# A fourth one-time place for an expert weight block, in room taken from the scratch of dynamic DMAs

## Chip, cores and metric

The kernel runs on one core of a Trainium2 chip. The metric is device time in microseconds (us) of one execution, taken as the median of several runs. The core has a matrix engine (TensorE, PE in the profile), three engines for elementwise work (VectorE or DVE, ScalarE or ACT, GpSimd or POOL) and SyncE (SP), which here only asks for DMA transfers. All transfers run on the core's 16 DMA engines between the large off-chip memory (HBM) and the on-chip memory (SBUF).

## What is computed

One inference step of a decoder layer for 256 prompt tokens and 8 sample tokens with width 1024: a combined projection, a gated delta rule for one group of heads and latent attention for the other, an output projection, cross attention over 256 memory tokens, and a mixture of 32 experts. Cut to the two stages that matter here:

```python
def cross_attend(hn, mem_k, mem_v, w_xq, w_xo):
    q = (hn @ w_xq).reshape(B, T, X_HEADS, X_HEAD_DIM)
    s = jnp.einsum('bthd,bmhd->bhtm', q, mem_k).astype(jnp.float32) * (X_HEAD_DIM ** -0.5)
    p = jax.nn.softmax(s, axis=-1).astype(mem_v.dtype)
    return jnp.einsum('bhtm,bmhd->bthd', p, mem_v).reshape(B, T, -1) @ w_xo

def moe_ffn(h, w_router, b_router, w_e1, b_e1, w_e2, b_e2):      # 32 experts, top 4
    ...
    def expert(acc, ew):
        hh = xt @ w1 + b1
        glu = jnp.minimum(hh[:, 0::2], SWIGLU_LIMIT)
        lin = jnp.clip(hh[:, 1::2], -SWIGLU_LIMIT, SWIGLU_LIMIT)
        y = ((lin + 1.0) * (glu * jax.nn.sigmoid(SWIGLU_ALPHA * glu))) @ w2 + b2
        return acc + g_col[:, None].astype(y.dtype) * y, None
```

For the 8 sample tokens, the cached keys and values of the latent attention are gathered through a page table, and each sample has its own cross-attention keys and values of 1 MB (`cache_mem_k`, `cache_mem_v`).

## The kernel before

The program is a chain of blocks with a barrier of all engines between them. Each engine's instructions are written out in order and tied to the others by semaphores. SBUF is one large tensor, `arena`, whose places are reused by hand, with a few small tensors beside it.

**Gathers.** `load_sequence` (L410) has POOL issue two indirect DMAs for each of 8 samples: the latent rows and the rotary-key rows, 128 descriptors each. Three places take the 8 sequences in turn, so a gather waits until the sequence before it in its place has been used.

**Cross attention of the samples** is in the last block (L1951). PE turns the keys of sample n into columns (`turn_keys`, two steps m for each sample, L2104) and scores them (`score`, L2112). Keys of samples 0 to 3 were loaded in the block before; those of samples 4 to 7 go into the same four places, and SP asks for each when the sample in its place has been scored (L1958). The expert biases are asked for between them (L1961, L1962), and then the values of samples 4 to 7 (L1965).

**Experts.** They go in 16 pairs. The weights of a pair are 24 fills of 1 MB each (128 partitions by 2048 floats): fills 0 to 15 are the first matrix of the two experts, 16 to 23 the second. Even fills belong to the first expert of the pair, odd ones to the second. PE uses them in order, two at a time: `hidden` (L2039) fills 0 to 15, `output` (L2076) fills 16 to 23. A pair takes 16 x 24 = 384 fills in all.

Fills go into a ring of 12 places. Three of the first pair's fills, 21 to 23, have one-time places outside the ring (`spare`, L1889), which other data holds before or afterwards. SP asks for the fills of the first pair as their places become free of earlier data: fill 0 in the block before, fill 3 as the first instruction of the last block (L1954), 8 to 11, 4 to 7, 1 and 2 as the cross attention gives up its buffers, 21 and 22 when the last projection is done, and 23 after the third set of router logits. From then on SP waits, before each fill, on the semaphore that PE raises when the place has been used:

```python
            for n in range(RING, FIRST_SPARE):
                sp.wait_ge(free[n % RING], 1)
                fill_first(sp, n)
            ...
            for n in range(RING):
                fill_later(1, n, 2)
```

`slot_of` and `uses` (L1910 to L1914) give the ring place of a fill in the later pairs and how often that place has been filled; both depend on `SPARE`, the number of one-time places.

Of the kernel before, what the change touches and what calls it, by code (L numbers as in the profile page):

```python
# [53 lines left out]
C_HEAD = C_SUB + 1  # L54
C_ALL = C_HEAD + H

ARENA = 45680

CACHED = (PAST // P) * (KVR + ROPE)
AT_WIN, AT_HEADS, AT_HIST = 0, 22528, 44032  # L60
# [82 lines left out]
def build(nc, x_prompt, x_sample, state_gdn, state_conv, cache_latent, cache_krope, page_table,  # L143
# [7 lines left out]
    def sem(name, lasting=False):  # L151
        s = nc.alloc_semaphore(name)
        if not lasting:
            recent.append(s)
        return s
# [7 lines left out]
    def keep(name, shape, dt=F32):  # L163
        return nc.alloc_sbuf_tensor(name, shape, dt)
# [4 lines left out]
    xnT = keep("xnT", [P, KD, TOK])  # L169
    arena = keep("arena", [P, ARENA])  # L170
    small = keep("small", [P, 64])
# [10 lines left out]
    def store(eng, dst, src):  # L182
        n_stored[0] += 16
        eng.dma_start(dst, src).then_inc(stored, 16)
# [260 lines left out]
    with nc.Block() as block:  # L445
        @block.sync
        def _(sp):
            for t in range(2):
                sp.dma_start(res[:, t, :], x_prompt[0, t * P:(t + 1) * P, :]).then_inc(tile_loaded[t], 16)
            sp.dma_start(res[0:DEC, 2, :], x_sample[:, 0, :]).then_inc(tile_loaded[2], 16)  # L450
            for k in range(KD):
                sp.dma_start(win[:, k, :], w_in[0, k * P:(k + 1) * P, :]).then_inc(w_in_loaded[k], 16)
            sp.dma_start(hist, state_conv[0].rearrange("b j c -> (b j) c")).then_inc(hist_loaded, 16)
            sp.dma_start(cst[:, P:C_ALL], const_f32[:, P:C_ALL]).then_inc(const_loaded, 16)

            sp.wait_ge(hist_moved, 1)
            sp.dma_start(pgi, page_table.rearrange("b j -> j b"), allow_slow_non_contiguous=True).then_inc(ml["pages"], 16)
            sp.dma_start(kvn[:, :], kv_norm[0].partition_broadcast(P)).then_inc(ml["kvn_loaded"], 16)
            sp.dma_start(alog[:, :], a_log[0].partition_broadcast(P)).then_inc(decay_loaded, 16)
            sp.dma_start(dtb[:, :], dt_bias[0].partition_broadcast(P)).then_inc(decay_loaded, 16)  # L460
            sp.dma_start(uq, w_uq[0].rearrange("(k p) h n -> p k h n", p=P)).then_inc(ml["uq_loaded"], 16)

            store(sp, conv_sample[0, :, 0:2, :], state_conv[0, :, 1:3, :])
            sp.wait_ge(tail_moved, 3)
            store(sp, conv_prompt[0, 0], tail[0:3, :])
            store(sp, conv_sample[0, :, 2, :], tail[3:3 + DEC, :])
            sp.wait_ge(ml["lat_ready"], NT)
            store(sp, lat_prompt[0, 0].rearrange("(t p) n -> p t n", p=P), rest[:, 0:2, CKV0:CKV0 + KVR])
            store(sp, lat_sample[:, 0, 0, :], rest[0:DEC, 2, CKV0:CKV0 + KVR])
            store(sp, kr_prompt[0, 0].rearrange("(t p) n -> p t n", p=P), kr[:, 0:2, :])  # L470
            store(sp, kr_sample[:, 0, 0, :], kr[0:DEC, 2, :])
            sp.wait_ge(rest_proj, 7)
            sp.dma_start(uk, w_uk[0].rearrange("(k p) h n -> p k h n", p=P)).then_inc(ml["w_loaded"], 16)
            sp.dma_start(uv, w_uv[0].rearrange("(k p) h n -> p k h n", p=P)).then_inc(ml["w_loaded"], 16)
            sp.wait_ge(stored, n_stored[0])
# [851 lines left out]
    AT_WK, AT_MEMT, AT_MV, AT_WOUT, AT_WV, AT_WXQ, AT_WXO = 0, 8192, 10240, 12288, 20480, 28672, 36864  # L1327
# [129 lines left out]
    def fill(sp, n, e, place, landed):  # L1457

        x = n % 2
        if n < 16:  # L1460
            k = n // 2
            src = w_e1[0, bass.ds(e + x, 1), k * P:(k + 1) * P, :].rearrange("a p n -> (a p) n")
            sp.dma_start(place, src).then_inc(landed, 16)
        else:
            k = 2 * ((n - 16) // 2)
            src = w_e2[0, bass.ds(e + x, 1), k * P:(k + 2) * P, :].rearrange("a (k p) n -> p (a k) n", p=P)
            sp.dma_start(place.rearrange("p (k n) -> p k n", k=2), src).then_inc(landed, 16)  # L1467

    def fill_first(sp, n):
        fill(sp, n, 0, ring[n % RING], full[n % RING])  # L1470
# [413 lines left out]
    AT_YE = late_moe.at  # L1884
    ye = late_moe.take([P, D])
    assert AT_YE + 2048 <= AT_WXO + KD * D
    SPARE = 3
    FIRST_SPARE = FILLS - SPARE
    spare = (xnT[:, :, :].rearrange("p k n -> p (k n)")[:, 0:2048], arena[:, AT_YE:AT_YE + 2048], arena[:, AT_WOUT + 2048:AT_WOUT + 4096])  # L1889
    spare_full = [sem(f"spare{i}_full") for i in range(SPARE)]  # L1890
    spare_used = sem("spare_used")
    left = (left_0, left_1, left_s)
# [17 lines left out]
    def slot_of(n):  # L1910
        return (n - SPARE) % RING

    def uses(it, n):
        return it * 2 + (n // RING + (0 if n % RING < SPARE else 1))  # L1914

# [22 lines left out]
    def wait_y(eng, it):  # L1938

        if type(it) is int and it == 0:  # L1940
            eng.wait_ge(spare_used, SPARE)
        else:
            eng.wait_ge(free[slot_of(23)], uses(it, 23))

    def n_rounds(eng):
        return eng.value_load(rounds[0:1, 0:1], min_val=1, max_val=MAXR)
# [4 lines left out]
    with nc.Block() as block:  # L1951
        @block.sync
        def _(sp):
            fill_first(sp, 3)  # L1954
            sp.wait_ge(stored, memory_stored)
            for b in range(G):
                sp.wait_ge(sx["scored"], b + 1)
                sp.dma_start(Kx[:, b], cache_mem_k[0, G + b].rearrange("(s p) h n -> p s (h n)", p=P)).then_inc(kx_loaded[b], 16)  # L1958
                if b > 0:
                    part = slice((b - 1) * NE, b * NE)  # L1960
                    sp.dma_start(bias[part, 0:2 * D], b_e1[0]).then_inc(mo["b_loaded"], 16)  # L1961
                    sp.dma_start(bias[part, 2 * D:3 * D], b_e2[0]).then_inc(mo["b_loaded"], 16)  # L1962
            for b in range(G):
                sp.wait_ge(sx["scored"], G + b + 1)
                sp.dma_start(Kx[:, b], cache_mem_v[0, G + b].rearrange("(s p) h n -> p s (h n)", p=P)).then_inc(kx_loaded[b], 16)  # L1965
            sp.dma_start(wr, w_router[0].rearrange("(k p) n -> p k n", p=P)).then_inc(mo["r_loaded"], 16)
            sp.dma_start(br, b_router[0].partition_broadcast(P)).then_inc(mo["r_loaded"], 16)
            sp.dma_start(pick, const_bf16).then_inc(mo["pick_loaded"], 16)
            sp.wait_ge(sx["out"], 1)
            for n in range(8, RING):  # L1970
                fill_first(sp, n)
            sp.wait_ge(sx["out"], 2)
            for n in range(4, 8):
                fill_first(sp, n)
            sp.wait_ge(mo["bias_ready"], 1)
            for n in (1, 2):
                fill_first(sp, n)
            sp.wait_ge(mo["made"], 5)
            for i in range(2):
                fill(sp, FIRST_SPARE + i, 0, spare[i], spare_full[i])  # L1980
            sp.wait_ge(mo["logits"], 3)
            fill(sp, FIRST_SPARE + 2, 0, spare[2], spare_full[2])

            sp.wait_ge(mo["rounds"], 1)
            sp.wait_ge(mo["parts_ready"], NT + 1)
            sp.dma_start(nf, norm_final.partition_broadcast(P)).then_inc(fn["gain"], 16)
            nr = n_rounds(sp)
# [4 lines that stand above are left out]
            def fill_later(it, n, e):  # L1992
                sp.wait_ge(free[slot_of(n)], uses(it, n) - 1)
                fill(sp, n, e, ring[slot_of(n)], full[slot_of(n)])

            for n in range(RING):
                fill_later(1, n, 2)
            with sp.Fori(1, nr * PAIRS - 1) as it:
                e = sp.snap((it % PAIRS) * 2)
                after = sp.snap(((it + 1) % PAIRS) * 2)  # L2000
                for n in range(RING, FILLS):
                    fill_later(it, n, e)
                for n in range(RING):
                    fill_later(it + 1, n, after)
            final = last_pair(sp)
            for n in range(RING, FILLS):
                fill_later(final, n, NE - 2)
            sp.wait_ge(fn["done"], 1)
            store(sp, y_sample[:, 0, :], res[0:DEC, 2, :])
            for t in range(2):  # L2010
                for n in range(2):
                    sp.wait_ge(fn["done"], 2 + 2 * t + n)
                    store(sp, y_prompt[0, t * P:(t + 1) * P, n * 512:(n + 1) * 512], res[:, t, n * 512:(n + 1) * 512])
            sp.wait_ge(stored, n_stored[0])
# [707 lines left out]
```

## Time and profile before

| | before |
|---|---|
| runs | 1494.47, 1496.4, 1496.8 us |
| median | 1496.4 us |
| profiled execution, span from first to last instruction | 1494.2 us |
| PE busy | 1373.9 us (92%) |
| moved by DMA | 490.73 MB, 328 GB/s over the span |

The page gives the profiled execution's span and no other time of it; the lowest of the runs is 0.3 us above that span, the median 2.2 us. Times in the rows are from the start of the span. SPq is SP's queue of DMA issues. The share of DMA is that of all 16 DMA engines; it can be over 1 in a short stretch, since packets are counted where they start.

### The profile page before, as it was taken

How to read it: one execution, taken by the hardware profiler on the slowest of the kernel's cores; microseconds unless marked ns; L12 is line 12 of the kernel's file. 1: busy time of each engine (PE TensorE's matmuls, PEld its weight loads, DVE VectorE, ACT ScalarE, POOL GpSimd, SP SyncE). 2: the span in 40 equal slices, each digit the busy share in tenths (PEclk: the TensorE clock that was granted, in tenths of full speed). 3: DMA queues.
4: the chain of work that ended last, by engine and by line, in shares of the span. 5: the costliest groups of instructions: out<-in, count | busy, mean ns of one | idle time of the engine just before them, and what ended most of it. 6: DMA issues, size and time to landing. Idle time of an engine off the chain costs nothing.

```text
span 1494.2 us, 21159 instructions
## 1 busy us (share of the span) xinstructions
PE 1373.9 (92%) x8579; PEld 694.5 (46%) x8579; DVE 460.2 (31%) x1116; ACT 201.1 (13%) x399; POOL 42.6 (3%) x37
## 2 busy tenths in 40 slices
PE   8999899899998989999999988989989889899896
PEld 7668766555486453333333333333433333333332
DVE  1856643553024252113113112111221131122213
ACT  1053322321012440000000000000000000000002
POOL 0000101000000320000000000000000000000000
PEclk9999999999999989999999999999999999999999
DMA  9111534448365669999999999999999999999996
GB/s 367 39 53 57 199 143 149 184 150 329 141 253 180 225 276 413 389 413 424 426 425 424 428 425 424 427 424 426 425 424 429 423 424 426 424 426 427 424 426 245
DMA packets 96727, 490.73 MB, mean 328 GB/s; under 512 B 9307, under 2 KB 14527, under 8 KB 61626
## 3 DMA queue, kind: packets, MB, share of 16 engines
q1 hardware_dynamic: 94074, 468.89, 76.8%
q0 software_dynamic: 2304, 20.97, 3.6%
q8 instruction: 39, 0.64, 0.2%
q10 hardware_dynamic: 296, 0.11, 0.0%
q14 instruction: 14, 0.11, 0.0%
HBM read 484.01 MB, written 6.04 MB: 328 GB/s over the span
## 4 chain that ended last, share of the span: by engine, by line
PE 40%; DMA 18%; DVE 6%; issue 2%; SPq 1%; ACT 1%; POOL 1%; DVEq 0%
PE ps L2039 17%; DMA arena<-in_w_e 17%; PE ps L2076 14%; PE ps L2032 2%; PE ps L2064 1%; DVE arena L2604 1%; DVE arena L2614 1%; DVE arena L2611 1%; PE ps L2088 1%; DVE arena L2612 1%; SPq L1467 1%; DMA arena<-in_cache_mem_k 1%; PE ps L2104 1%; PE ps L2118 1%; PE ps L2112 0%
## 5 line engine op out<-in xcount | busy, mean ns | idle before, releaser
L2039 PE MATMUL ps<-arena 128*64 128x512 f32 x2048 | 454.3, 595 | 22.1 <-DMA arena<-in_w_e 21.5
L2039 PEld LDWEIGHTS ps<-arena 128*64 128x64 f32 x2048 | 148.9, 137 | 303.5 <-issue 278.5
L2076 PE MATMUL ps<-arena 128*64 128x512 f32 x952 | 214.2, 604 | 2.4 <-ACT arena L2291 2.4
L2076 PEld LDWEIGHTS ps<-arena 128*64 128x64 f32 x952 | 77.9, 141 | 136.1 <-issue 123.3
L2611 DVE TENSOR_SCALAR arena<-ps 128x1024 f32<-128x1024 f32 x15 | 18.4, 1225 | 243.5 <-PE ps L2039 243.5
L2032 PE MATMUL ps<-arena 96*128 96x512 bf16 x96 | 35.3, 488 | 46.0 <-DVE arena L2604 46.0
L2623 DVE COPY arena<-ps 128x512 f32<-128x512 f32 x15 | 10.4, 692 | 216.5 <-PE ps L2076 216.5
L2629 DVE TENSOR_TENSOR res<-res,ps 128x512 f32<-128x512 f32 x60 | 41.3, 688 | 115.9 <-PE ps L2088 115.9
L2025 PEld LDWEIGHTS ps<-arena 128*128 128x128 bf16 x768 | 49.5, 99 | 14.0 <-issue 12.2
L1753 PE MATMUL ps<-arena 128*128 128x512 f32 x128 | 55.8, 594 | 0.0
L2025 PE MATMUL ps<-arena 128*128 128x128 bf16 x768 | 54.0, 222 | 1.7 <-DVE arena L2578 1.7
L2088 PE MATMUL ps<-arena 128*128 128x512 f32 x120 | 55.5, 605 | 0.0
L2289 ACT ACTIVATE arena<-arena 128x1024 f32<-128x1024 f32 x15 | 15.9, 1057 | 293.5 <-DVE arena L2611 293.5
L1107 ACT COPY arena<-ps 128x384 f32<-128x384 f32 x64 | 30.6, 478 | 98.7 <-PE ps L1035 98.1
L2595 DVE TENSOR_SCALAR arena<-cst,arena 128x64 bf16<-128x64 f32 (+1 forms) x90 | 22.2, 247 | 62.2 <-PE ps L2056 62.2
L1095 DVE COPY arena<-ps 128x256 f32<-128x256 f32 x64 | 26.8, 423 | 44.5 <-PE ps L1039 41.0
L2293 ACT COPY arena<-ps 128x512 f32<-128x512 f32 x15 | 8.8, 587 | 218.1 <-PE ps L2076 218.1
L1753 PEld LDWEIGHTS ps<-arena 128*128 128x128 f32 x128 | 24.0, 190 | 29.2 <-issue 29.1
L2088 PEld LDWEIGHTS ps<-arena 128*128 128x128 f32 x120 | 21.6, 189 | 33.7 <-issue 33.7
L2032 PEld LDWEIGHTS ps<-arena 96*128 (+1 forms) x96 | 9.7, 115 | 55.4 <-issue 49.0
L538 PE MATMUL ps<-arena,xnT 128*128 128x392 f32 (+2 forms) x96 | 35.3, 525 | 0.0
L2286 ACT COPY arena<-ps 128x256 f32<-128x256 f32 x15 | 5.6, 373 | 219.6 <-PE ps L2056 219.6
(553 smaller groups left out, 1533.0 us busy)
## 6 DMA issues: line engine op xcount, KB each, us to landing
arena<-in_w_e SPq DMA_DIRECT2D x383, 1024.0 KB, 18.0
arena<-in_w_in SPq DMA_DIRECT2D x8, 1380.0 KB, 17.6
arena<-in_cache_mem_k SPq DMA_DIRECT2D x8, 1024.0 KB, 8.9
arena<-in_w_out SPq DMA_DIRECT2D x2, 2048.0 KB
arena<-in_w_xk SPq DMA_DIRECT2D x1, 4096.0 KB, 15.9
arena<-in_w_xv SPq DMA_DIRECT2D x1, 4096.0 KB, 13.8
arena<-in_w_xq SPq DMA_DIRECT2D x1, 4096.0 KB, 23.2
arena<-in_cache_mem_v SPq DMA_DIRECT2D x1, 4096.0 KB, 16.1
```

The costliest lines, as they stand in the source:

```text
L538: last = pe.matmul(ps[:, bank, 0:b - a], xnT[:, k, cols(t)], win[:, k, CONV + a:CONV + b], start=(k == 0), stop=(k == KD - 1))
L1095: nc.vector.tensor_copy(KT[:, k % 2, p, 3 * P:5 * P], ps[:, key_banks(k, p)[1], 0:2 * P]).then_inc(sa["odd_moved"], 1)
L1107: nc.scalar.copy(KT[:, k % 2, p, 0:3 * P], ps[:, key_banks(k, p)[0], 0:3 * P]).then_inc(sa["even_moved"], 1)
L1753: last = pe.matmul(ps[:, i % 4, :], memT[:, k, cols(t)], w[:, k, n * 512:(n + 1) * 512], start=(k == 0), stop=(k == KD - 1))
L2025: pe.matmul(out, xp[:, t, i, k * P:(k + 1) * P], picked[:, t, :], start=(t == 0 and i == 0), stop=False)
L2032: pe.matmul(ps[:, bank, :], mine, b1[:, a + i * 512:a + (i + 1) * 512], start=True, stop=True)
L2039: last = pe.matmul(ps[64 * x:64 * x + 64, c, :], xe[:, k, 64 * x:64 * x + 64], weights[x][:, c * 512:(c + 1) * 512], start=False, stop=(k ...
L2076: last = pe.matmul(ps[64 * x:64 * x + 64, 4 + c, :], aT[:, k, 64 * x:64 * x + 64], weights[x][:, j * D + c * 512:j * D + (c + 1) * 512], s ...
L2088: pe.matmul(ps[:, COMBINE_BANKS[2 * t + c], :], gT[:, t, :], ye[:, c * 512:(c + 1) * 512], start=True, stop=True).then_inc(lp["combined"], 1)
L2595: last = nc.vector.tensor_scalar(picked[0:q, t, 64 * x:64 * x + 64], io, slot[0:q, t, place], None, ALU.is_equal)
L2611: nc.vector.tensor_scalar(glu[:, :].rearrange("p (c n) -> p c n", c=4), hid[:, :, :, 0], 7.0, None, ALU.min).then_inc(lp["glu"], 1)
L2629: nc.vector.tensor_tensor(a, a, ps[:, COMBINE_BANKS[i], :], ALU.add).then_inc(lp["added"], 1)
```

## The change

The scratch that is set aside in each SBUF partition for the descriptors of dynamic DMAs goes from its default size to 4096 bytes, a quarter of it. `arena` grows by the difference, 3072 floats in each partition, and the last 2048 of them become a fourth one-time place. It takes fill 20 of the first pair, which was in the ring before (place 8, asked for after fill 8 had been used). It is free from the start, and SP asks for fill 20 as the first instruction of the last block, ahead of fill 3. Fills 21 to 23 keep their places and their times. All fills of later pairs move by one place in the ring.

```diff
-ARENA = 45680
+ARENA = 45680 + 3072
+SCRATCH = 4096
...
-    SPARE = 3
+    SPARE = 4
     FIRST_SPARE = FILLS - SPARE
-    spare = (xnT[:, :, :].rearrange("p k n -> p (k n)")[:, 0:2048], arena[:, AT_YE:AT_YE + 2048], arena[:, AT_WOUT + 2048:AT_WOUT + 4096])
+    spare = (arena[:, ARENA - 2048:ARENA], xnT[:, :, :].rearrange("p k n -> p (k n)")[:, 0:2048], arena[:, AT_YE:AT_YE + 2048], arena[:, AT_WOUT + 2048:AT_WOUT + 4096])
...
         @block.sync
         def _(sp):
+            fill(sp, FIRST_SPARE, 0, spare[0], spare_full[0])
             fill_first(sp, 3)
...
             sp.wait_ge(mo["made"], 5)
-            for i in range(2):
+            for i in range(1, 3):
                 fill(sp, FIRST_SPARE + i, 0, spare[i], spare_full[i])
             sp.wait_ge(mo["logits"], 3)
-            fill(sp, FIRST_SPARE + 2, 0, spare[2], spare_full[2])
+            fill(sp, FIRST_SPARE + 3, 0, spare[3], spare_full[3])
...
-    nc = bacc.Bacc("TRN2", target_bir_lowering=False, num_devices=1)
+    nc = bacc.Bacc("TRN2", target_bir_lowering=False, num_devices=1, dynamic_dma_scratch_size=SCRATCH)
```

## Rows read from the trace of the kernel before

**Rows 1.** The page: what the DMA engines moved in 40 equal slices.
```profile
GB/s 367 39 53 57 199 143 149 184 150 329 141 253 180 225 276 413 389 413 424 426 425 424 428 425 424 427 424 426 425 424 429 423 424 426 424 426 427 424 426 245
```

**Rows 2.** Chain that ended last, in order of time: start us, us, what.
```profile
475.02 11.93 DMA arena<-in_cache_mem_k
487.00 1.09 PE ps L2104 x8
...
555.96 10.52 PE ps L2039 x48
...
843.44 21.96 DMA arena<-in_w_e
...
1459.31 18.35 DMA arena<-in_w_e
```

**Rows 3.** PE's waits from 555 to 700 us, all: total, times, longest.
```profile
PE ps L2032 <- DVE arena L2604: 6.0, 2, 3.1
PE ps L2039 <- DVE arena L2604: 0.6, 1, 0.6
PE ps L2076 <- ACT arena L2291: 0.4, 1, 0.4
```

**Rows 4.** PE's waits from 700 us to the end, the one on weights.
```profile
PE ps L2039 <- DMA arena<-in_w_e: 21.5, 22, 1.2
```

**Rows 5.** SP's DMA issues in order: start us, us, line, out<-in, count.
```profile
462.01 0.34 SPq L1463 DMA_DIRECT2D arena<-in_w_e  x1
466.19 3.26 SPq L1958 DMA_DIRECT2D arena<-in_cache_mem_k  x2
...
559.64 4.24 SPq L1463 DMA_DIRECT2D arena<-in_w_e  x4
566.51 7.91 SPq L1467 DMA_DIRECT2D arena<-in_w_e  x5
574.46 42.38 SPq L1463 DMA_DIRECT2D arena<-in_w_e  x16
623.70 11.90 SPq L1467 DMA_DIRECT2D arena<-in_w_e  x8
638.17 35.40 SPq L1463 DMA_DIRECT2D arena<-in_w_e  x16
```

**Rows 6.** Windows of half a microsecond: busy time by engine, PE clock, DMA share, GB/s.
```profile
624.00:624.50 0.50, 0.50 (x5) 0.21 (x6) 0.24 (x2) 0.40 (x2) 0.00 (x0) 1.00 0.17 66
...
656.50:657.00 0.50, 0.50 (x6) 0.23 (x4) 0.00 (x0) 0.00 (x0) 0.00 (x0) 1.00 0.37 82
```

**Rows 7.** One window from 658 us to the last fill's landing.
```profile
658.00:1478.00 820.00, 752.81 (x3896) 298.94 (x3894) 177.84 (x342) 38.99 (x73) 0.00 (x0) 0.98 1.01 424
```

**Rows 8.** Windows at the start of the last block.
```profile
462.00:466.00 4.00, 3.94 (x41) 3.01 (x41) 2.07 (x3) 1.76 (x3) 0.95 (x1) 1.00 0.67 246
466.00:468.00 2.00, 2.00 (x24) 1.79 (x23) 0.70 (x2) 0.59 (x2) 0.00 (x0) 1.00 0.51 82
468.00:487.00 19.00, 14.07 (x153) 10.10 (x153) 6.91 (x10) 5.86 (x10) 0.00 (x0) 1.00 1.02 317
```

**Rows 9.** PE's waits from 455 to 560 us, those on the keys.
```profile
PE ps L2104 <- DMA arena<-in_cache_mem_k: 4.9, 2, 3.2
```

**Rows 10.** The page: the queue of the gathers; packets, MB, share.
```profile
q0 software_dynamic: 2304, 20.97, 3.6%
```

**Rows 11.** The gathers of sequence 1 on POOL, and PE's first use of it.
```profile
154.24 1.05 POOL L412 DMA_INDIRECT arena<-in_cache_latent,arena  x1 [44.32 <-POOLq L160]
155.59 0.95 POOL L412 DMA_INDIRECT arena<-in_cache_krope,arena  x1 [0.30 <-issue]
...
172.66 0.44 PE L1033 MATMUL ps<-cst,arena 128*128 128x128 f32 x2
```

**Rows 12.** Gathers to landing: latent rows asked at 150 to 157 us; all rotary-key rows.
```profile
DMA to landing us min/median/max: 13.3/15.8/18.3
...
DMA to landing us min/median/max: 8.2/9.2/18.5
```

## The prediction

> **What bounds the kernel now.** The slices of the page come first: from the fifteenth slice on, some 560 us into the span, the DMA engines move 389 to 429 GB/s until the last slice, at 424 to 429 in nearly all of them, and before that far less [rows 1]. A kernel whose second half runs at one steady rate of transfers looks bound by them there. The chain of waits refines that: it goes through PE's matmuls from 556 us on, and weights appear in it only from 843 us, up to the last fill at 1459 + 18.35 = 1477.7 us [rows 2]. PE's waits say the same: from 555 to 700 us PE waits 7.0 us in all, on VectorE and ScalarE and never on weights [rows 3], and all its 21.5 us of waiting on weights in L2039 come after 700 [rows 4].
>
> So there are two regimes, and for one transfer less the border between them decides. Until the border PE sets the time: the ring is full and SP waits for PE to free a place. After it, the DMA engines never rest and set the end by themselves. Find the border by counting fills. When PE has used c fills, c at least 24, the three one-time places are spent and SP can have asked for 12 + c at most. SP's issues make 15 + 4 + 5 + 16 = 40 fills by 616.8 us, the next only at 623.70 [rows 5]; in the half microsecond from 624.00 the DMA engines carry 66 GB/s instead of some 425 [rows 6]. All 40 have landed: c is 28 (the first pair and four fills of the second), and the ring is full. Eight more issues end at 635.6 and the batch from 638.17 begins [rows 5]; its first four bring 52, the bound for c = 40, which is where PE stops using weights to turn the expert's activations. At 656.5 us the rate falls to 82 GB/s [rows 6]: those 52 have landed too. There is no such hole afterwards: 424 GB/s as a mean from 658 to 1478 us [rows 7]. The count closes: 384 - 52 = 332 fills of 1.0486 MB at 424 GB/s are 821 us, and 657 + 821 = 1478. The end is the moment at which PE frees the first places of the second pair's second matrix, near 655 us, plus 332 transfers, plus the 16 us from 1478 to the span's end.
>
> **The change part by part.** *Fill 20 leaves the ring.* At 424 to 426 GB/s one fill is 2.47 us of transfer. It goes out of the stretch from 560 us on, so all later fills of the first pair can be asked for one use earlier: 16 + c in place of 15 + c while c is at most 20. But the fourth place is used once, like the other three. At c = 24 the bound is 36 with either kernel, at 28 it is 40, at 40 it is 52. The holes at 624 and 656 us are the DMA engines waiting for PE with everything landed; with one transfer less before them they wait longer. From the second hole on, the same 332 fills are left, and their start hangs on PE, which had waited on no weights until then [rows 3]. The saving goes into idle time of the DMA engines: 0 us. If the holes were not real (a few engines dry and the others behind), up to all 2.47 us would be saved; that is the lower end. I take 0, as the rate in the holes is a fifth of the full one or less.
>
> The Trainium skill speaks for the change here: in "DMA: Bandwidth & Descriptors", section "Rules for kernel authors", it says to ask for a DMA early and wait on its semaphore late. By that rule the sum would be 2.47 us less; rows 6 show the place where this case departs from it, since the transfer taken away was not what the end waited for.
>
> *The transfer appears at 462 us.* SP's first DMA issue of the block takes 0.34 us, and the next wait of SP ends only at 466.19 [rows 5], so what SP does is hidden; that cover is 3.8 us wide. The DMA engines are the point. Fill 3 starts there, and from 466 to 468 us they are partly idle: 82 GB/s times 2 us is 0.16 MB where 426 GB/s would carry 0.85 MB, so 0.69 MB or 1.6 us of transfer are free [rows 8]. From 468 to 487 us they are at a share of 1.02, full (at 317 GB/s, as the biases come in short rows) [rows 8]. Fill 20 and fill 3 go ahead in the same queue; of the 2.46 us that fill 20 needs, 1.6 fit into the gap, and 0.86 us push the keys of sample 4 back. The queue never empties before 487, so the keys of sample 7 come 0.86 us later too, and for those PE waits: 4.9 us in two waits [rows 9], the last of which ends the chain's step from 475.02 with its landing at 487.0 [rows 2]. That is on the path: what follows (the scores, the casts of the biases, the projection, the router, the first pair at 555.96) has no other start. Bounds: 0 if the keys' landing were set by something other than the queue, 2.46 us if the gap at 466 us is a delay that reappears behind fill 20. I take 0.86, the value that the windows give.
>
> *This is not paid back.* Pair 0 begins 0.86 us later, so do PE's uses, so does the restart near 656 us, and with it the end.
>
> *The scratch.* Only the gathers on POOL use dynamic descriptors of this kind: 2304 packets for 16 gathers [rows 10], 144 each, 9 on each of 16 DMA engines. No gather is longer if its descriptors have room. I take 0. The most it could cost is in the rivals. *The rest:* SP issues as many DMAs as before; the other edits change indices only, and every fill keeps its size. *Moved addresses* of the small tensors and `arena`: no row shows that an address matters; 0.
>
> Sum on the profiled execution: 1494.2 + 0.86 - 0 = 1495.1 us. The median of the runs is 2.2 us over that span, so 1496.4 + 0.86 gives 1497.3 us.
>
> **Rivals.** *Hidden on both sides.* The keys are not delayed in a way that PE sees, and the saving is lost as above: 1496.4. For it: the gap at 466 us might be wider for a queue that is never empty. Against it: the share of 1.02 right behind.
>
> *The credit is real.* The holes are only partly holes, and the DMA stream ends up to 2.47 us earlier: 1496.4 + 0.86 - 2.47 = 1494.8, or 1493.9 without the delay of the keys. For it: at 656.5 us the share is still 0.37 [rows 6]. Against it: 624 us, with 66 GB/s, lies earlier and is already behind c = 24.
>
> *The whole transfer delays the keys:* 1496.4 + 2.46 = 1498.9. For it: the queue is one, and fill 20 is first in it. Against it: the free 0.69 MB.
>
> *The smaller scratch makes POOL wait* (the other side: slower). If it held the descriptors of one gather at a time, the rotary keys of sequence 1 could be asked for only when its latent rows have landed, 154.24 + 13.3 = 167.5 us instead of 155.59, and with the median landing of 9.2 us come at 176.7, 4.0 us after PE starts that sequence at 172.66 [rows 11, 12]; with the longest of 18.5 us [rows 12] it would be 13 us. The median gives 1497.3 + 4.0 = 1501.3 us. It decides once fewer than 18 descriptors on each engine fit at a time. Later gathers have a spare place to run ahead in and would stay hidden. Against it: with three places for the sequences at most six gathers are open at once, 54 descriptors on an engine; for it: no row shows how many fit.
>
> The Trainium skill bears on this one: "DMA: Bandwidth & Descriptors", section "Terms", gives a descriptor 16 bytes and puts the rings of software-made descriptors in SBUF. As an estimate from that page, 4096 bytes of a partition are 256 descriptors, above the 144 that rows 10 give for the whole run; by it this rival has no price, and the trace of before can't show the ring's size.
>
> **How the numbers follow.** The forecast, a delay of the keys near 0.86 us with no credit, gets 0.50; hidden on both sides 0.15; the credit, whole or in part, 0.17; the whole delay 0.12; the scratch 0.04; something unseen 0.02. A measurement of this kernel tells about 0.2% (3.0 us) from no change; its three runs lie 2.3 us apart. All cases but the scratch end within 2.5 us of before, so "same" holds nearly all: 0.87. Faster by more gets 0.04 (the full credit with a favourable measurement), slower 0.09 (the scratch, and the whole delay with an unfavourable one). The range takes in the full credit and the whole delay: 1494.0 to 1499.4.
>
> **What would show it.** In the changed profile: two issues at 462 us (L1467, L1463); 2 MB at full rate until about 468.7 with no gap at 466; PE's last wait on keys ending near 487.9; the first pair at 556.8; after c = 24 a wider hole at 624 us and again some 3.5 us wide before 657.5; the steady stream from 658.5 to 1478.6; POOL's gathers as they were. The forecast is wrong if the hole before 657 us does not widen, if the first matmul of the pairs isn't later, or if the rate of the stream after it is other than 424 GB/s.

## The result and the profile after

The changed kernel takes 1499.78 us in the median of 22 runs, the kernel before, beside it, 1495.84 us: a ratio of 1.0027 with a 95% interval of 1.0016 to 1.0038, 4.0 us slower by that ratio. Two more timings of the changed kernel gave 1.0018 (0.9996 to 1.0041) and 1.0031 (1.0014 to 1.0047). The forecast was 1497.3 us and "same"; the direction was right, the size (0.9 us) about a fifth of what came.

The profiled execution has a span of 1503.0 us, at the upper end of the runs. Its chain of waits, start us, us, what, beside [rows 2]:

```profile
477.07 17.87 DMA arena<-in_cache_mem_k
494.99 1.97 PE ps L2106 x8
...
565.15 10.52 PE ps L2041 x48
...
1468.25 18.22 DMA arena<-in_w_e
```

(Lines behind the change stand one or two further down than in the kernel before.) The last wait for keys ends at 494.99 where it ended at 487.00, and the pairs begin at 565.15 instead of 555.96. From there to the end it is 937.8 us, before it was 938.2. Nothing is lost or won in the stream of weights; all the time goes before it. Some of the 9.2 us are not the change's: the block itself begins 2.1 us later, and that start lies anywhere from 457 to 468 us in the profiles, up to 4.1 us apart for one and the same kernel. What is left, 7.1 us, lies between the block's first matmul and the first matmul of the pairs, which is the measure for all that follows: 93.9 us before, 101.0 here.

PE's waits on keys were 4.9 us in two [rows 9]:

```profile
PE ps L2106 <- DMA arena<-in_cache_mem_k: 8.1, 3, 3.6
```

The windows that answer to [rows 8] (busy by engine, PE clock, DMA share, GB/s) and one in the last keys:

```profile
464.00:468.00 4.00, 3.89 (x40) 3.00 (x40) 2.07 (x3) 1.76 (x3) 0.95 (x1) 1.00 0.73 233
468.00:470.00 2.00, 2.00 (x20) 1.75 (x17) 0.69 (x1) 0.59 (x1) 0.00 (x0) 1.00 1.06 442
470.00:495.00 25.00, 16.91 (x154) 11.67 (x153) 6.92 (x10) 5.87 (x10) 0.00 (x0) 0.85 1.02 255
495.50:496.00 0.50, 0.50 (x4) 0.50 (x3) 0.00 (x0) 0.00 (x0) 0.00 (x0) 0.50 1.02 418
```

Three things are to be seen. The gap at 466 us is gone, as forecast: from 468 to 470 the engines are full. In the stretch behind it they are full too, but carry 255 GB/s where they carried 317: the same work takes longer, not only starts later. And the granted clock of PE, 0.85 as a mean there, is 0.50 (1.2 GHz) after the last wait: the eight turns of keys at 494.99 take 1.97 us, those at 487.00 in [rows 2] 1.09 us.

The holes of the DMA stream, beside [rows 6 and 7], are where the saving went:

```profile
621.50:622.00 0.50, 0.50 (x5) 0.19 (x3) 0.00 (x0) 0.00 (x0) 0.00 (x0) 1.00 0.00 0
...
664.50:665.00 0.50, 0.50 (x4) 0.16 (x2) 0.00 (x0) 0.00 (x0) 0.00 (x0) 1.00 0.04 16
667.00:1487.00 820.00, 762.94 (x3898) 302.95 (x3895) 177.91 (x342) 39.03 (x73) 0.00 (x0) 0.95 1.01 424
```

57 us after the pairs' start the DMA engines stand still, with nothing to fetch; after the second hole the stream runs at the same 424 GB/s for the same 820 us. The kernel before had a dip at that place too, which the prediction passed over: also 57 us after its pairs' start, just behind c = 24, and not empty.

```profile
613.00:613.50 0.50, 0.50 (x6) 0.24 (x4) 0.00 (x0) 0.00 (x0) 0.00 (x0) 1.00 0.32 131
```

So it is this dip that widened; the hole at 624 us that the prediction named lies at 633 us now and is no wider than it was.

The gathers follow one another as before, 1.35 us apart (start us, us, engine, line), so the smaller scratch holds POOL up nowhere:

```profile
155.39 1.05 POOL L413 DMA_INDIRECT arena<-in_cache_latent,arena  x1 [44.15 <-POOLq L161]
156.74 1.04 POOL L413 DMA_INDIRECT arena<-in_cache_krope,arena  x1 [0.30 <-issue]
```

### The profile page after: what moved, and what is told of

Same layout as the page of the kernel before. It is cut to its first block, busy times and chain, and to the rows that moved or that the text cites. A ratio compares the mean times of both kernels' runs of the same rounds, so it can differ in the third digit from the quotient of the medians.

```text
span 1503.0 us, 21189 instructions
## 1 busy us (share of the span) xinstructions
PE 1389.9 (92%) x8579; PEld 700.6 (47%) x8579; DVE 460.7 (31%) x1116; ACT 201.4 (13%) x399; POOL 42.7 (3%) x37
## 4 chain that ended last, share of the span: by engine, by line
PE 47%; DMA 12%; DVE 6%; issue 2%; SPq 1%; ACT 1%; POOL 1%; DVEq 0%
PE ps L2041 22%; PE ps L2078 14%; DMA arena<-in_w_e 10%; PE ps L2034 2%; PE ps L2090 2%; PE ps L2066 2%; DVE arena L2606 1%; DVE arena L2616 1%; DVE arena L2613 1%; DMA arena<-in_cache_mem_k 1%; DVE arena L2614 1%; SPq L1468 1%; PE ps L2106 1%; PE ps L2120 1%; PE ps L2114 0%
## 5 line engine op out<-in xcount | busy, mean ns | idle before, releaser
L2034 PE MATMUL ps<-arena 96*128 96x512 bf16 x96 | 42.0, 568 | 45.9 <-DVE arena L2606 45.9
L2625 DVE COPY arena<-ps 128x512 f32<-128x512 f32 x15 | 10.4, 692 | 222.4 <-PE ps L2078 222.4
## 6 DMA issues: line engine op xcount, KB each, us to landing
arena<-in_cache_mem_k SPq DMA_DIRECT2D x8, 1024.0 KB, 10.4
```

The source lines that it names most:

```text
L2034: pe.matmul(ps[:, bank, :], mine, b1[:, a + i * 512:a + (i + 1) * 512], start=True, stop=True)
```

## The experiments

Ratios are to the kernel before on the same chip, with 95% intervals. "Keys" is the time from issue to landing of the keys of samples 4 to 7, "to pairs" the measure above, "on" from the pairs to the span's end; all from each run's one profile.

| run | ratio | keys, us | to pairs | on |
|---|---|---|---|---|
| before | | 4.9, 6.1, 8.6, 11.9 | 93.9 | 938.2 |
| before_2 | 0.9999 (0.9982 to 1.0017) | 5.1, 6.3, 8.7, 12.0 | 91.4 | 939.1 |
| after | 1.0027 (1.0016 to 1.0038) | 6.4, 10.2, 14.2, 17.9 | 101.0 | 937.8 |
| after_again | 1.0018 (0.9996 to 1.0041) | 6.5, 8.6, 11.3, 14.5 | 97.5 | 938.4 |
| after_3 | 1.0031 (1.0014 to 1.0047) | 7.3, 8.8, 11.8, 14.4 | 96.0 | 939.4 |
| e1_scratch | 1.0000 (0.9982 to 1.0018) | 5.4, 6.8, 9.4, 11.6 | 91.2 | 938.6 |
| e2_late | 1.0006 (0.9986 to 1.0027) | 4.9, 6.0, 8.6, 11.8 | 91.4 | 939.5 |
| e5_swap | 0.9998 (0.9978 to 1.0018) | 5.0, 6.2, 9.1, 12.4 | 93.3 | 938.8 |
| e4_half_more | 1.0033 (1.0012 to 1.0053) | 7.5, 8.8, 11.5, 13.4 | 97.6 | 938.0 |
| h1_busy | 1.0012 (1.0000 to 1.0024) | 7.1, 8.7, 11.7, 14.4 | 94.7 | 938.2 |
| f1_before_bias | 0.9958 (0.9942 to 0.9973) | 5.0, 5.2, 6.0, 6.3 | 87.4 | 937.5 |
| bias_behind_2 (same kernel) | 0.9964 (0.9947 to 0.9981) | 5.1, 5.4, 5.7, 5.8 | 88.6 | 938.2 |
| e3_bias_behind | 0.9997 (0.9983 to 1.0011) | 7.2, 6.8, 6.5, 6.3 | 87.2 | 938.1 |
| bias_behind_fill20_2 (same kernel) | 0.9991 (0.9970 to 1.0012) | 6.2, 6.5, 7.8, 10.4 | 93.6 | 937.1 |
| g1_bias_later | 1.0002 (0.9986 to 1.0018) | 5.1, 5.3, 5.5, 5.1 | 94.5 | 937.9 |
| g2_bias_later_fill20 | 1.0017 (1.0000 to 1.0035) | 6.6, 6.7, 7.6, 7.3 | 101.1 | 938.3 |
| f2_before_bias_first | 0.9968 (0.9954 to 0.9982) | 6.2, 6.6, 6.8, 6.4 | 86.8 | 938.5 |
| clean_3_places (same kernel) | 0.9953 (0.9931 to 0.9976) | 5.7, 5.6, 6.0, 5.5 | 87.4 | 937.2 |
| g3_fill20_clean | 0.9949 (0.9934 to 0.9963) | 5.8, 5.7, 6.0, 5.5 | 87.3 | 939.4 |
| clean_4_places (same kernel) | 0.9956 (0.9937 to 0.9974) | 6.6, 6.4, 6.3, 5.8 | 87.4 | 936.9 |

**One part alone.** The scratch and the longer `arena` without the fourth place:

```diff
+ARENA = 45680 + 3072
+SCRATCH = 4096
...
     SPARE = 3
```

> The scratch at a quarter and arena longer, and nothing else: three one-time places as before, fill 20 in the ring, the new room unused. Theory A (the early fill 20 delays the keys of samples 4 to 7): the time of before within 0.1%, first matmul of the block to first matmul of the pairs 93.9 us as before. Rival B (the smaller scratch or the moved addresses cost the time): about 4 us or 0.27% slower with the early stages longer, the gathers of sequence 1 asked later than 1.35 us after one another. Rival C (the loss is in the stream of weights): not touched here, so the time of before.

Ratio 1.0000, 91.2 us to the pairs: scratch and addresses cost nothing that this interval (0.9982 to 1.0018) shows, and rival B, which wants 1.0027 and longer early stages, falls.

Fill 20 in its new place, but asked for later:

```diff
-            fill(sp, FIRST_SPARE, 0, spare[0], spare_full[0])
             fill_first(sp, 3)
...
             sp.dma_start(pick, const_bf16).then_inc(mo["pick_loaded"], 16)
+            fill(sp, FIRST_SPARE, 0, spare[0], spare_full[0])
```

> The changed kernel with fill 20 asked for after the keys, the values, the router and the pick table instead of first. Theory A: the keys come as before, PE's last wait on them ends 24.9 us after the block's first matmul (30.9 in the changed kernel), the pairs start 93.9 us after it, and the saving of one transfer is lost in the holes of the DMA stream: ratio to before 1.000, between 0.999 and 1.001. Rival B (scratch): ratio 1.0027 as with the whole change. Rival D (the credit of 2.47 us is real once the keys are not delayed): 2.5 us faster, ratio 0.9983.

Ratio 1.0006, 91.4 us, keys to 0.1 us as before: in the profile the whole loss goes with the moment at which fill 20 is asked for. The timing agrees, though its interval alone, up to 1.0027, wouldn't settle it. The credit isn't there either: 939.5 us from the pairs on.

Fill 20 first and fill 3 late, so that 1 MB is ahead of the keys as before:

```diff
             fill(sp, FIRST_SPARE, 0, spare[0], spare_full[0])
-            fill_first(sp, 3)
...
             sp.dma_start(pick, const_bf16).then_inc(mo["pick_loaded"], 16)
+            fill_first(sp, 3)
```

> The changed kernel with fill 20 first and fill 3 moved to where the pick table has been asked for, so that 1 MB is ahead of the keys, as before the change. Theory A (volume ahead of the keys): first matmul of the pairs 91.2 to 93.9 us after the block's first, waits on the keys of 3 to 5 us, ratio 0.999 to 1.001. Rival F (it is fill 20 itself, with its 4 KB rows or its place, that delays the keys, not the volume): 97 to 101 us and ratio 1.0027.

Ratio 0.9998 (0.9978 to 1.0018) and 93.3 us. It is a second megabyte ahead of the keys that costs, and not fill 20 as such: rival F falls.

**More volume.**

```diff
+            sp.dma_start(arena[:, 45680:46704], w_e2[0, 0, 0:P, :]).then_inc(more_full, 16)
             fill(sp, FIRST_SPARE, 0, spare[0], spare_full[0])
             fill_first(sp, 3)
```

> The changed kernel with another transfer of 0.5 MB ahead of fill 20, into the 1024 floats of the new room that are left over; its data is not used. Theory A: more ahead of the keys, more delay: at least 1.2 us above the changed kernel, by the same factor as fill 20 cost (7.1 us in its profiled execution or 4.0 us between the medians, for 2.47 us of transfer) 2 to 3.5 us, so 6 to 8 us above before, ratio 1.004 to 1.005. Rivals B and C (scratch, or stream): as the changed kernel, 1.0027.

A miss: 1.0033, at most a little above the changed kernel, and the last keys landed 13.4 us after their issue, no later than with fill 20 alone. The waits of PE were spread over four keys here, 7.0 us in all, and SP asks for each key as an earlier one is scored (its last issue came 13.9 us after the block's first matmul, 13.0 in after and after_again), so part of the delay shows in the issue. The same happened in after_3, where the last issue came 13.7 us after the block's first matmul: in these two PE waits for the keys of sample 4 already (0.7 us here, 0.5 in after_3), and it turns the first half of them before it scores sample 3, which SP waits for. The cost does not grow in proportion.

**Second and third profile of the changed kernel, and a second of the unchanged.**

> The changed kernel once more, for a second profile. Theory A: what it loses lies between the block's first matmul and the first matmul of the pairs, which is 91.2 to 93.9 us apart where nothing stands ahead of fill 3: here 95 to 101 us, and from the pairs to the end 937.8 to 939.5 us as in all the others; ratio to before 1.0016 to 1.0038. Rival E (the first profile showed a rare execution and the loss of 4 us lies elsewhere): 91 to 94 us there, and the difference in another stretch.

> The kernel before once more, as the first of four on one chip: without and with fill 20 first, each with the biases between the keys and behind them. Theory A: pairs 91 to 94 us after the block's first matmul, ratio 1.000. It gives a second profile of the unchanged kernel.

> The changed kernel, second of the four. Theory A: pairs 97 to 101 us after the block's first matmul, ratio 1.0018 to 1.0038. Rival E (the profiles were chance): 91 to 94 us.

97.5 and 96.0 us, against 93.9 and 91.4 us in the two profiles of the kernel before; the first profile, with 101.0, was at the far end. The 96.0 lies just below the 97 to 101 that were expected, and far from rival E's 91 to 94. What a usual execution looks like: PE's turns of keys in after_3, start us, us, idle before and its releaser:

```profile
476.78 1.09 PE L2106 MATMUL ps<-cst,arena 128*128 128x128 f32 x8 [0.53 <-DMA arena<-in_cache_mem_k]
...
481.16 1.09 PE L2106 MATMUL ps<-cst,arena 128*128 128x128 f32 x8 [1.26 <-DMA arena<-in_cache_mem_k]
...
487.10 1.09 PE L2106 MATMUL ps<-cst,arena 128*128 128x128 f32 x8 [2.83 <-DMA arena<-in_cache_mem_k]
488.13 1.93 PE L2114 MATMUL ps<-arena 128*32 128x256 f32 x16
489.99 1.82 PE L2106 MATMUL ps<-cst,arena 128*128 128x128 f32 x8
...
493.37 1.10 PE L2106 MATMUL ps<-cst,arena 128*128 128x128 f32 x8 [1.56 <-DMA arena<-in_cache_mem_k]
```

and in before_2:

```profile
481.37 1.09 PE L2104 MATMUL ps<-cst,arena 128*128 128x128 f32 x8 [1.84 <-DMA arena<-in_cache_mem_k]
482.39 1.89 PE L2112 MATMUL ps<-arena 128*32 128x256 f32 x16
484.21 1.90 PE L2104 MATMUL ps<-cst,arena 128*128 128x128 f32 x8
487.67 1.09 PE L2104 MATMUL ps<-cst,arena 128*128 128x128 f32 x8 [1.56 <-DMA arena<-in_cache_mem_k]
```

All four late keys are waited for now, 6.2 us instead of 3.4. The doubled durations (1.93 and 1.82 us for what takes 1.07 and 1.09) are stretches at 1.2 GHz behind a wait: the granted clock is 0.54 as a mean from 488.13 to 491.80 in after_3. They occur before the change too (0.54 from 482.39 to 486.10 in before_2). Where they fall decides their price: ahead of another wait for keys they cost nothing here, since the keys come no earlier. Behind the last one they are all paid: from the end of the last turn to the pairs it is 63.3 to 64.8 us in every profile but those of g1 and g2 below (which wait for the biases), so what makes that turn late makes the pairs late. From the first to the last turn of the last sample's keys it is 2.85 us at 2.4 GHz and 5.31 at 1.2; it was 5.31 in after, after_again and e4_half_more (and in bias_behind_fill20_2 below), 2.85 in after_3, and in the five profiles with 1 MB ahead of mixed keys 4.36 once and 2.84 or 2.85 four times.

**PE kept busy in the waits.**

```diff
                 n, s = m // 2, m % 2
+                if m in (10, 12, 14):
+                    for i in range(16):
+                        pe.transpose(ps[:, 7, 0:P], ident, ident)
                 if s == 0:
```

> The changed kernel with 16 extra transposes of the identity on PE, some 1.8 us, ahead of the waits for the keys of samples 5, 6 and 7; their result is not used. If a part of the cost is PE's clock, which falls after it has idled: the granted clock of the 37 us from the block's first matmul is 0.95 or more (0.82 to 0.95 in the changed kernel), the stretch from the first to the last matmul on the keys of sample 7 is 2.85 us and not 5.3, and the ratio falls by 0.0005 to 0.0015 against the changed kernel, to 1.0015 to 1.0025. If the clock is no part of it: the ratio stays at 1.0027 or goes up.

The window of 37 us from the block's first matmul, in after and in h1_busy:

```profile
464.11:501.11 37.00, 28.51 (x240) 20.11 (x240) 10.73 (x16) 9.16 (x16) 0.91 (x1) 0.82 0.95 266
```

```profile
462.74:499.74 37.00, 33.59 (x314) 24.54 (x315) 12.17 (x20) 12.70 (x21) 2.15 (x8) 1.00 0.99 314
```

With needless work the clock stays at 1.00, the last turns take 2.84 us, and the ratio is 1.0012, though the keys land as late as in the changed kernel (14.4 us for the last). The difference to 1.0027 is some 2 us, to the 1.0018 of after_again 0.9 us. That fits a share of the clock and does not show one: the intervals overlap, and 1.0012 lies just below the 1.0015 to 1.0025 that were expected.

**Keys without biases among them.** First with the biases moved behind the last key, in the changed kernel and in the one before, each twice:

```diff
-                if b > 0:
-                    part = slice((b - 1) * NE, b * NE)
-                    sp.dma_start(bias[part, 0:2 * D], b_e1[0]).then_inc(mo["b_loaded"], 16)
-                    sp.dma_start(bias[part, 2 * D:3 * D], b_e2[0]).then_inc(mo["b_loaded"], 16)
+            for b in range(1, G):
+                part = slice((b - 1) * NE, b * NE)
+                ...
             for b in range(G):
                 sp.wait_ge(sx["scored"], G + b + 1)
```

> The changed kernel, fill 20 first, with the three pairs of bias loads moved from between the keys to behind the last of them. Theory A1 (fill 20 costs much more than its 2.46 us of transfer because it makes keys and biases stand in the queue together, and packets of both run at half the rate while mixed): keys of sample 7 land within 9 us of their issue instead of 17.9, PE waits under 2 us on keys instead of 8.1, the ratio to before is 0.997 to 1.000. Rival A2 (the delay is the plain 1 MB ahead of the keys, whatever stands between them): the wait on the keys shrinks only by what the biases take themselves, some 4 us of transfer at 200 GB/s, and stays above that of before, 4.9 us.

> The kernel before with the bias loads moved from between the keys to behind the last of them; beside the same move in the changed kernel (waits on the keys 0.4 us, pairs 87.2 us after the block's first matmul). Theory A1 (mixing of keys and biases multiplies the delay): without the mixing fill 20 costs next to nothing, so this lies within 1 us of that run: pairs at 86 to 88 us, no wait on keys, ratio 0.996 to 0.999. Rival A2 (a plain 1 MB): 2.5 us earlier than that run.

> The kernel before with the biases behind the keys, third of the four. Both theories: as in its first run, ratio 0.994 to 0.997, pairs 86 to 88 us after the block's first matmul, no wait on keys.

> The changed kernel with the biases behind the keys, fourth of the four. Theory A1 (fill 20 is dear only where keys and biases are mixed): within 1 us of the third, ratio 0.994 to 0.997. Rival A2 (fill 20 costs some 4 us with or without the mixing, and the first profile of this kernel showed a lucky execution): ratio 0.998 to 1.001, and waits on the keys of 1 to 4 us in the profile.

The first pair of profiles spoke for A1 (87.2 and 87.4 us), while the timings, 0.9997 and 0.9958, spoke against it. On one chip the four kernels gave 0.9999 and 1.0031 with mixing, 0.9964 and 0.9991 without: fill 20 costs 0.003 either way, so A1 as I had put it fell, and what A2 expected came (0.998 to 1.001, waits on keys of 1 to 4 us: 0.9991 and 3.3 us). The first profile with fill 20 was a lucky one. In the second the first two keys land 6.2 and 6.5 us after their issue and the last after 10.4; the first of the biases, asked for 0.4 us behind that key, lands 3.3 us before it.

So the biases went further back, to the second value load:

> The kernel before with the biases asked for after the second of the value loads. Theory A: keys unmixed, each lands 5 to 6 us after its issue, no wait on keys, pairs 86 to 89 us after the block's first matmul, ratio 0.994 to 0.997.

> The changed kernel with the same move. Theory A1 (where no biases stand among or right behind the keys, the queue catches up and fill 20 costs next to nothing): keys land 7.2, 6.8, 6.5 and 6.3 us after their issue or sooner, waits on keys under 1 us, ratio within 0.0015 of the kernel without fill 20. Rival A2 (the plain transfer costs its 2.5 us or more anyway): last key over 8 us after its issue, ratio 0.0025 or more above the kernel without.

Now the keys come nearly as A1 says: 6.6, 6.7, 7.6 and 7.3 us after their issue with fill 20, where A1 had 7.2, 6.8, 6.5 and 6.3 at most, and waits of 0.7 us. The first matmul on the last sample's keys is 20.6 us after the block's first, against 19.7: 0.9 us. That this is the prediction's figure is chance. The last key itself lands 2.2 us later than without fill 20 (20.2 us after the block's first matmul, 18.0 in g1), but PE's other work covers that; the 0.9 us come from the wait for the key before it. My ratio for g1 and its 86 to 89 us to the pairs (94.5 came) were wrong, since the biases are late now: ScalarE waits 2.35 us for them in g1 and 8.0 us in g2. With fill 20 the queue as a whole is late, and whatever stands last in it is waited for. The ratios of the two differ by 0.0015, on A1's bound, so they decide nothing.

**The biases first, fill 3 late, with three and with four places.**

```diff
-            fill_first(sp, 3)
             sp.wait_ge(stored, memory_stored)
+            for b in range(1, G):
+                part = slice((b - 1) * NE, b * NE)
+                ...
             for b in range(G):
...
             sp.dma_start(pick, const_bf16).then_inc(mo["pick_loaded"], 16)
+            fill_first(sp, 3)
```

> The kernel before with the biases asked for first in the block, ahead of the keys, and fill 3 after the pick table. Theory A: the biases use DMA time that was partly idle, and the keys come unmixed; pairs 86 to 88 us after the block's first matmul, waits on keys under 1 us, ratio 0.996 to 0.998. Rival (the biases, some 6 us of transfer at 190 GB/s, delay the first key as fill 20 did): waits of 2 us or more on the keys of samples 4 and 5, ratio 1.000.

> The changed kernel with the biases first in the block, and fill 20 and fill 3 after the pick table; beside the same kernel with three one-time places (ratio 0.9968, 938.5 us from the first matmul of the pairs to the end). Theory A (the transfer that leaves the ring was not what the end waited for): 937 to 939.5 us from the pairs to the end, ratio 0.995 to 0.998. Rival D (credit of 2.47 us once nothing is delayed): 936 us, ratio 0.993 to 0.995.

> The kernel before with the biases first and fill 3 after the pick table, once more, beside the same kernel with fill 20 in a fourth one-time place. Ratio 0.995 to 0.997, 937 to 939.5 us from the first matmul of the pairs to the end.

> The same with fill 20 in the fourth one-time place, asked for after the pick table. Theory A (no credit): ratio within 0.001 of the kernel with three places, 937 to 939.5 us from the pairs to the end. Rival D (credit of 2.47 us): 0.0017 below it, 935 to 937 us.

No key is waited for in any of these, and on one chip three places give 0.9953 and four 0.9956. With intervals of 0.002 either way that alone does not exclude a credit of 2.47 us, and g3's 0.9949 lies in rival D's range. The stretch from the pairs to the end decides: it is 938.2 us as a mean of the eight profiles with three places and 938.3 of the twelve with four, where a credit would make it 2.47 us shorter. So a fourth place is worth nothing here. Four windows of 1 us from 54 us after the pairs' start, first with three places, then with four:

```profile
609.00:610.00 1.00, 1.00 (x8) 0.49 (x6) 0.00 (x0) 0.00 (x0) 0.00 (x0) 1.00 0.99 418
610.00:611.00 1.00, 1.00 (x8) 0.38 (x5) 0.00 (x0) 0.00 (x0) 0.00 (x0) 1.00 1.10 467
611.00:612.00 1.00, 1.00 (x7) 0.35 (x4) 0.00 (x0) 0.00 (x0) 0.00 (x0) 1.00 0.95 401
612.00:613.00 1.00, 1.00 (x8) 0.49 (x6) 0.00 (x0) 0.00 (x0) 0.00 (x0) 1.00 0.90 205
```

```profile
601.40:602.40 1.00, 1.00 (x8) 0.49 (x6) 0.00 (x0) 0.00 (x0) 0.00 (x0) 1.00 0.59 246
602.40:603.40 1.00, 1.00 (x8) 0.37 (x5) 0.00 (x0) 0.00 (x0) 0.00 (x0) 1.00 0.12 49
603.40:604.40 1.00, 1.00 (x7) 0.35 (x5) 0.00 (x0) 0.00 (x0) 0.00 (x0) 1.00 0.00 0
604.40:605.40 1.00, 1.00 (x8) 0.48 (x6) 0.00 (x0) 0.00 (x0) 0.00 (x0) 1.00 0.68 123
```

The missing transfer is there to be seen as DMA engines at rest. Between 50 and 62 us after the pairs' start they carry less than at a steady 425 GB/s would be carried, by 0.5 to 1.1 us of transfer in the profiles with three places and by 2.9 to 3.6 us in those with four: all of the 2.47 us is there. Both kernels beat the one before and the changed one, by some 6 to 7 us against before in this timing, 5 and 8 us in the others (f2_before_bias_first, g3_fill20_clean). They change two things, the place of the biases and that of fill 3; the biases alone gave the same gain in f1_before_bias.

## Why the prediction was wrong

- **The border between the regimes and the count of fills held.** In all 20 profiles it is 936.9 to 939.5 us from the pairs' start to the end, whatever happened before. The credit of 2.47 us went into the holes, as forecast, but not into the hole that the prediction named (624 us): into the dip 55 to 57 us after the pairs' start, where c has just passed 24. The rival of a real credit fell by e2_late and by the stretch from the pairs to the end in all profiles. That goes against the rule of the Trainium skill ("DMA: Bandwidth & Descriptors", section "Rules for kernel authors") to issue a DMA early and wait on it late: asked for early, fill 20 cost a ratio of 1.0027 (after), asked for late 1.0006 (e2_late).
- **The scratch and the other edits at 0 held** (e1_scratch).
- **The step that failed** is the term "0.86 us push the keys of sample 4 back. The queue never empties before 487, so the keys of sample 7 come 0.86 us later too". The mechanism was right, place and sign too: more bytes ahead of the keys make the keys late, and PE waits for them. The size was not. In bytes the term came out: the block's first 3.15 MB have been moved 9.3 us after its first matmul in after and after_3 (9.7 in after_again); in the kernel before the first 2.10 MB had been moved at 8.4 us, 0.9 us earlier. But the term makes the keys' landing follow from that moment, as if transfers landed one after another in the order asked. They don't. The first key came 1.2 to 2.2 us later, counted from its issue, with fill 20 ahead than without, in the kernels with the biases moved away as well, so mixing with them is not the reason. The last key landed 24.9 and 25.0 us after the block's first matmul in the two profiles of before, and 27.4, 28.0 and 30.8 in the three of the changed kernel: 2.5 us or more later, the whole transfer at least, and not what the gap left over. A later transfer can land ahead of an earlier one: in after the first bias, asked for 0.4 us behind the last key, landed 2.1 us before it (asked to landing: key, then two biases).

```profile
arena<-in_cache_mem_k SPq DMA_DIRECT2D x1, 1024.0 KB, 17.9
arena<-in_b_e SPq DMA_DIRECT2D x1, 256.0 KB, 15.3
arena<-in_b_e SPq DMA_DIRECT2D x1, 128.0 KB, 17.9
```

It did so before the change too (9.6 us from issue to landing against the key's 11.9). So a count of the bytes asked for ahead of a key does not give its landing. From 6 us after the block's first matmul to the last key's landing the engines carried 318 and 310 GB/s before, 255, 282 and 272 after, at a share near 1 all the time: a full share does not say that the same work takes the same time when the queue is longer. Why the first key's lateness grows from key to key stays open. Where the biases had been moved away it did so in some executions only: the last key's time from issue to landing was longer with fill 20 by nothing (e3_bias_behind), 2.2 us (g2_bias_later_fill20) and 4.6 us (bias_behind_fill20_2).
- **Smaller misreadings.** The biases do not come in short rows: their packets are of 8 and 4 KB, those of the keys of 4 KB. The fast slices of [rows 1] begin with the sixteenth (413 GB/s), the fifteenth has 276. Neither changes the sum.
- **The clock was put at nothing, so the bound of 2.46 us was no bound.** The sum left out what an idle PE costs afterwards: up to 2.46 us more when the clock is at 1.2 GHz behind the last wait (5.31 against 2.85 us). The rival in which the whole transfer delays the keys had the key's part nearly right and was given 0.12; with the clock's part its time would have been 1498.9 to 1501.3 us.
- The two terms together, some 2.5 us or more for the last key and 0 to 2.5 us for the clock, make 2.5 to 5 us; between the medians it was 3.9 and 3.8 us in the two larger timings and 2.9 in the third. How often the clock falls behind the last wait was seen in a few profiles only, so the split is not settled; h1_busy, 2 us below one timing of the changed kernel and 0.9 below another, points to a half of it or less.

## What to carry to other kernels

A transfer asked for early is free only if nothing that is waited for stands behind it in the queue: look at the first late landing after the new place, not at the idle share there. Count places and uses before adding a buffer: a place that is used once gives its lead back at the first moment when the ring is full. And price a longer wait of PE with the slower clock behind it; where a kernel waits for loads anyway, the order of those loads (here the biases among the keys) was worth more than the place.

## What the runs showed of the hardware

The loads of the biases, which go to 32 partitions, slow those they stand among. With the DMA engines at a share of 0.94 to 1.04 the stretches with biases in them carry little (a window of after):

```profile
492.50:493.00 0.50, 0.00 (x0) 0.00 (x0) 0.00 (x0) 0.00 (x0) 0.00 (x0) 1.00 0.94 147
```

Single packets show it. A packet of 4 KB of the keys took 159 ns in the median from 468 to 470 us of before, and 308 ns from 483 to 486, with biases in flight. One of 8 KB took 309 ns in fill 3 and 634 ns in the biases of f2_before_bias_first, which carried 225 GB/s at a share of 1.01 with nothing among them. That the 32 partitions are the reason, and not something else about these loads, was not tested.

With the biases out of the keys' way the last key lands 5.8 to 6.3 us after its issue instead of 11.9 to 12.0 (f1_before_bias, bias_behind_2). And the start of the last block, some 462 us after the span's start, wanders by 11 us between profiles, over several chips and kernels (456.7 to 467.8), by up to 4.1 us within one and the same kernel, while the 938 us behind the pairs' start hold within 2.7 us: with that spread a change of 4 us takes some twenty runs to see, and one profile's span says little.
